# Moving the gate projection of a state-space block into the steps of its scan, with smaller edits to the attention before it

## The reference, cut to what matters

```
s_lat = einsum(q, k) * scale + bias;  s_lat = where(valid, s_lat, -1e30)
p = softmax(concat([s_lat, s_ctx, (sink)]));  out = p_lat @ v + p_ctx @ v_ctx
```

```
u = rmsnorm(h);  lru_x, lru_g, z, xbc, dt = split(u @ w_in)
xbc = silu(causal_conv(xbc));  xs, B, C = split(xbc);  dt = softplus(dt + bias)
y = ssd_scan(xs, dt, -exp(a_log), B, C) + xs * D
g = y * silu(z);  g = g * rsqrt(mean(g*g over each group of 512) + eps) * w
h = h + concat([y_a, g]) @ w_out
```

## Time and profile before

| what | us |
|---|---|
| median of three runs (3709.3 to 3714.8) | 3712.28 |
| the profiled execution, its own time | 3710.25 |
| its span, first to last instruction | 3708.5 |
| mean granted TensorE clock | 0.969 of full |

### The profile page before, as it was taken

How to read it: one execution, slowest core, us unless ns; L and a number is a source line. 1 busy time by engine, 2 the same in 40 slices (tenths; PEclk the granted TensorE clock), 3 DMA queues, 4 the chain that set the end, 5 groups by cost and what they waited for, 6 DMA issues and landing times.

```text
span 3708.5 us, 52151 instructions
## 1 busy us (share of the span) xinstructions
PE 3490.8 (94%) x19951; PEld 3021.8 (81%) x19951; DVE 2211.7 (60%) x3314; ACT 1434.8 (39%) x2472; POOL 724.3 (20%) x299
## 2 busy tenths in 40 slices
PE   7899999988999999999999998899998889979998
PEld 4899997855789999889999785778888789669776
DVE  6888885158288888788888617431226544551065
ACT  4433333147353333453333416542223623321274
POOL 1011111200211111111111230234442134023402
PEclk9999999999999999999999999999998999879999
DMA  5333333110133333333333320123332122012301
GB/s 222 107 121 122 124 104 119 59 46 1 45 140 121 117 119 120 116 119 114 114 114 108 120 74 34 46 69 97 96 102 86 40 79 86 12 46 80 97 7 57
DMA packets 94532, 333.57 MB, mean 90 GB/s; under 512 B 12272, under 2 KB 14576, under 8 KB 93424
## 3 DMA queue, kind: packets, MB, share of 16 engines
q1 hardware_dynamic: 91248, 316.28, 25.6%
q10 hardware_dynamic: 3072, 14.40, 1.1%
HBM read 322.12 MB, written 8.52 MB: 89 GB/s over the span
## 4 chain that ended last, share of the span: by engine, by line
PE 61%; issue 23%; POOL 6%; DVE 6%; ACT 2%; DMA 1%; SPq 0%; POOLq 0%; DVEq 0%; ACTq 0%
PE psum L2374 23%; PE psum L2253 14%; PE psum L2233 13%; POOL w_parts L682 6%; PE psum L2288 1%; PE psum L2131 1%; PE psum L2477 1%; PE psum L2583 1%; DVE normed L1323 1%; PE psum L2680 1%; PE psum L2711 1%; PE psum L2725 1%; PE psum L2707 1%; PE psum L2451 0%; DMA const<-const_dram 0%
## 5 line engine op out<-in xcount | busy, mean ns | idle before, releaser
L682 POOL TENSOR_TENSOR w_parts<-w_raw,w_parts 128x1024 fp32r<-128x1024 f32 x289 | 705.4, 2442 | 2880.7 <-ACT w_parts L722 2867.7
L2233 PE MATMUL psum<-h_parts,w_parts 128*128 128x264 f32 (+1 forms) x5712 | 958.0, 330 | 36.7 <-DVE to_split L1932 10.9
L2233 PEld LDWEIGHTS psum<-h_parts,w_parts 128*128 128x128 f32 x5712 | 854.9, 191 | 135.1 <-issue 34.6
L722 ACT ACTIVATE w_parts<-w_raw 128x1024 fp32r<-128x1024 f32 x283 | 300.1, 1061 | 1113.0 <-PE psum L2233 712.8
L2253 PE MATMUL psum<-w_parts,hidden_parts 128*128 128x512 f32 x2904 | 670.4, 392 | 14.7 <-DVE hidden_parts L1283 7.8
L2253 PEld LDWEIGHTS psum<-w_parts,hidden_parts 128*128 128x128 f32 x2904 | 546.8, 189 | 133.8 <-issue 12.7
L2374 PE MATMUL psum<-h_parts,w_parts 128*128 128x384 f32 x2880 | 531.2, 336 | 16.5 <-ACT y_tok L873 14.1
L2374 PEld LDWEIGHTS psum<-h_parts,w_parts 128*128 128x128 f32 x2880 | 504.5, 189 | 20.4 <-issue 16.9
L892 ACT ACTIVATE w_parts<-psum 128x512 fp32r<-128x512 f32 x240 | 143.8, 599 | 368.3 <-PE psum L2374 145.2
L2374 PE MATMUL psum<-h_sums,w_parts 128*128 128x384 f32 x1440 | 268.9, 334 | 0.0
L2374 PEld LDWEIGHTS psum<-h_sums,w_parts 128*128 128x128 f32 x1440 | 251.3, 188 | 0.0
(11 more groups left out here) (362 smaller groups left out, 4163.7 us busy)
## 6 DMA issues: line engine op xcount, KB each, us to landing
w_raw<-wu_dram SPq DMA_DIRECT2D x295, 512.0 KB, 3.6
mod_ring<-modw_dram SPq DMA_DIRECT2D x128, 512.0 KB, 4.5
w_raw_pairs<-wg_dram SPq DMA_DIRECT2D x120, 512.0 KB, 3.7
kept_dram<-resid SPq DMA_DIRECT2D x2, 3136.0 KB, 9.9
resid<-kept_dram SPq DMA_DIRECT2D x16, 392.0 KB, 5.7
na_bias<-rpb_dram ACTq DMA_DIRECT2D x6, 896.0 KB, 4.8
four_dft<-four_dram ACTq DMA_DIRECT2D x2, 2048.0 KB, 8.3
mod_first_k<-modw_dram SPq DMA_DIRECT2D x7, 512.0 KB, 10.0
```

Of the source, the lines that this page charges most:

```text
L682: pool.tensor_tensor(SPL[:, s % 2, 1], RAW[:, s % 2], SPL[:, s % 2, 0].bitcast(F32), ALU.subtract).then_inc(w_split, 1)
L722: act.activation(SPL[:, u % 2, 0], RAW[:, u % 2], ACT.Copy).then_inc(w_hi, 1)
L2233: ins = pe.matmul(PS[:, pair, PSO[a]:PSO[a] + z - a], w[:, wp, k], src[:, xp, k, t0 + a:t0 + z], start=k == 0 and n_ == 0, stop=k == KT - ...
```

## The change

1. The eight units of z leave their place ahead of the preparation. Each is run as two halves of 264 tokens in scan steps 0 to 7: PE runs the first half after `from_state` and the second after `outputs`, each in one PSUM bank (banks 2 and 3). The decays rotate over two banks instead of three.
2. Silu of z becomes: ACT takes tanh(z/2) into `ZT`, DVE computes (tanh + 1)*z into `Z`, and the gate multiplies by 0.5. The silu instructions and their waits go; a table load for exp and tanh is requested after the last silu of `xbc`.
3. Gating, squares and square sums leave steps 1 to 10 and are done in step 8 (tiles and groups 0 to 3), step 9 (4 to 7) and step 10 (8 and 9), since all of `Z` is needed first.
4. Attention: the row maximum is written negated (`negate=True`), and line 1712 goes.
5. Attention: POOL, not DVE, adds the masks to the second and third bias table of each layer (two instructions a table), after it has split the first 18 units of the layer.

```diff
+    GATE_STEPS = {8: (0, 1, 2, 3), 9: (4, 5, 6, 7), 10: (8, 9)}
...
+            def bias_masks(sub):                                     # POOL
+                mx = sub["in"]["mix"]
+                pool.wait_ge(tab_in, 64 * (mx + 1))
+                for ot in (1, 2):
+                    pool.wait_ge(tb_in[ot % 2], 16 * (mx + 1 if ot == 1 else 2 * mx + 2))
+                    tb = TB[:, ot % 2].rearrange("p x (n r c) -> p x n r c", n=7, r=8)
+                    for x in range(2):
+                        pool.tensor_tensor(tb[:, x], tb[:, x], MASKS[:, 0:7 * NA_C]...broadcast_to([P, 7, 8, NA_C]), ALU.add).then_inc(s_bias, 1)
...
-                for j in unit_steps(u, 8):                            # ACT
-                    act.activation(row2(Z[:, j]), two(u + j), ACT.Silu).then_inc(silu_ready, 1)
-                u += 8
+                act.preload_act_table_set("exp_and_others")
...
+                def z_tanh_half(n):
+                    if n % 2 == 0:
+                        act.wait_ge(z_half, n // 2 + 1)
+                    else:
+                        act.wait_ge(unit_done, u + n // 2 + 1)
+                    if n >= 2:
+                        act.wait_ge(z_read, n - 1)
+                    act.activation(ZT[:, n % 2], bank(2 + n % 2, T2 // 2), ACT.Tanh, scale=0.5).then_inc(z_tanh, 1)
+                decays(*SSD_STEPS[0])
                 for c in range(11):
-                    if c < 10:
-                        decays(*SSD_STEPS[c])
-                    if c >= 1:
-                        gated_squares(*SSD_STEPS[c - 1])
+                    if c < 8:
+                        z_tanh_half(2 * c)
+                    if c < 9:
+                        decays(*SSD_STEPS[c + 1])
+                    if c < 8:
+                        z_tanh_half(2 * c + 1)
+                        high_part(u, 0, c + 2)
+                    for d in GATE_STEPS.get(c, ()):
+                        gated_squares(*SSD_STEPS[d])
...
-                        step(dve.reduce_max(SM[:, a % 2, 0, :], sb[:, :, lo:1 + w + CTX], AX_X))       # DVE
-                        dve.tensor_scalar(SM[:, a % 2, 1, :], SM[:, a % 2, 0, :], -1.0, None, ALU.mult).then_inc(s_max, 1)
+                        dve.reduce_max(SM[:, a % 2, 0, :], sb[:, :, lo:1 + w + CTX], AX_X, negate=True).then_inc(s_max, 1)
...
+                def gate(c, i, g, a, z):
                     dve.wait_ge(y_read, c + 1)
-                    dve.tensor_tensor(x, x, Z[:, 4 * g:4 * g + 4, a:z], ALU.mult).then_inc(gated, 1)
+                    dve.scalar_tensor_tensor(x, x, 0.5, Z[:, 4 * g:4 * g + 4, a:z], ALU.mult, ALU.mult).then_inc(gated, 1)
+                def z_silu_half(n):
+                    j, w = n // 2, T2 // 2
+                    dve.wait_ge(z_tanh, n + 1)
+                    dve.scalar_tensor_tensor(Z[:, j, n % 2 * w:n % 2 * w + w], ZT[:, n % 2], 1.0, bank(2 + n % 2, w),
+                                             ALU.add, ALU.mult).then_inc(z_read, 1)
...
+                    if 1 <= c <= 8:
+                        z_silu_half(2 * c - 1)
                     if c >= 1:
                         gated_out(*SSD_STEPS[c - 1])
+                    if c == 8:
+                        dve.wait_ge(z_read, 16)
+                    for d in GATE_STEPS.get(c, ()):
+                        gate(*SSD_STEPS[d])
                     if c < 8:
+                        z_silu_half(2 * c)
                         dve.wait_ge(s_mm_, c + 1)
...
-                loop_units(u, 2, H2, T2, [(pad_ready, PRIME + 17 + j) for j in range(4)], (silu_ready, SI2 + 8))   # PE
-                u += 8
-                pe.wait_ge(silu_ready, SI2 + 16)
+                pe.wait_ge(pad_ready, PRIME + 20)
...
+                def z_unit_half(n):
+                    j, w = n // 2, T2 // 2
+                    if n % 2 == 0:
+                        pe.wait_ge(w_split, u + j + 1)
+                    if n >= 2:
+                        pe.wait_ge(z_read, n - 1)
+                    parts, a = SPL[:, (u + j) % 2], n % 2 * w
+                    for k in range(DT):
+                        for n_, (wp, xp) in enumerate(((0, 0), (0, 1), (1, 0))):
+                            ins = pe.matmul(bank(2 + n % 2, w), parts[:, wp, k], H2[:, xp, k, a:a + w],
+                                            start=k == 0 and n_ == 0, stop=k == DT - 1 and n_ == 2)
+                    ins.then_inc(unit_done if n % 2 else z_half, 1)
...
                     if c < 9:
                         decays(*SSD_STEPS[c + 1])
                         from_state(*SSD_STEPS[c + 1])
+                    if c < 8:
+                        z_unit_half(2 * c)
                     if c < 10:
                         to_state(*SSD_STEPS[c])
                         outputs(*SSD_STEPS[c])
-                    if c >= 1:
-                        square_sums(*SSD_STEPS[c - 1])
+                    if c < 8:
+                        z_unit_half(2 * c + 1)
+                    for d in GATE_STEPS.get(c, ()):
+                        square_sums(*SSD_STEPS[d])
```

More of the change, by code:

```diff
@@ L206, in build @@
     ST = place("stats", [P, 4, 8], F32)
-    SM = place("softmax_stats", [P, 2, 4, 2], F32)
+    SM = place("softmax_stats", [P, 2, 3, 2], F32)
     LAM = place("lru_rates", [P, 8, 8], F32, a_cond)
@@ L235, in build @@
     COLS = place("ssd_cols", [P, 4, 5, HEADS], F32, a_arena + 47680)
+    ZT = place("z_tanh_half", [P, 2, T2 // 2], F32, LOW)
     XDT = place("ssd_xdt", [P, 5, D], F32, a_y)
@@ L329, in build @@
     four_a_s, four_ev, four_b_s = sem("four_a"), sem("four_read"), sem("four_b")
+    s_bias = sem("bias_masked")
     s_lat, s_out, vf_ready, vf_rows = sem("score_bias"), sem("pv_read"), sem("v_features_ready"), sem("v_rows_mm")
@@ L347, in build @@
         sem("ssd_gated"), sem("ssd_sq_ready"), sem("ssd_sq_summed"))
+    z_half, z_tanh, z_read = sem("z_half_mm"), sem("z_tanh"), sem("z_half_read")
     ssd_const, tile_diag, tile_decay_mm = sem("ssd_const"), sem("ssd_tile_diag"), sem("ssd_tile_decay_mm")
@@ L692, in low_parts @@
                     low_part(u + s, s)
+            def bias_masks(sub):
[5 more added lines that the diff above has]
+                    for x in range(2):
+                        pool.tensor_tensor(tb[:, x], tb[:, x], MASKS[:, 0:7 * NA_C].rearrange("p (n c) -> p n c", n=7).unsqueeze(2)
+                                           .broadcast_to([P, 7, 8, NA_C]), ALU.add).then_inc(s_bias, 1)
             u = 0
             for sub in subs:
+                if sub["kind"] == "mix":
+                    start = sub["in"]["u"] + 18
+                    low_parts(u, start - u)
+                    bias_masks(sub)
+                    u = start
                 if sub["fo"] is None:
@@ L1686, in mix @@
                         sb, w, ot = SB[:, a % 3], st["w"], st["ot"]
-                        if st["na"] and st["t"] == 0:
-                            dve.wait_ge(tb_in[ot % 2], 16 * (mx + 1 if ot == 1 else 2 * mx + 1 + ot // 2))
+                        if st["na"] and st["t"] == 0 and ot > 0:
+                            dve.wait_ge(s_bias, 4 * mx + 2 * ot)
+                        if st["na"] and st["t"] == 0 and ot == 0:
+                            dve.wait_ge(tb_in[0], 16 * (2 * mx + 1))
                             for x in range(2):
@@ L1716, in mix @@
                         dve.wait_ge(s_exp, a + 1)
-                        step(dve.reciprocal(SM[:, a % 2, 3, :], SM[:, a % 2, 2, :]))
+                        step(dve.reciprocal(SM[:, a % 2, 2, :], SM[:, a % 2, 1, :]))
                         for x in range(2):
                             sb = SB[:, a % 3, x, 1:1 + w]
-                            dve.tensor_scalar(sb, sb, SM[:, a % 2, 3, x:x + 1], None, ALU.mult).then_inc(s_norm, 1)
+                            dve.tensor_scalar(sb, sb, SM[:, a % 2, 2, x:x + 1], None, ALU.mult).then_inc(s_norm, 1)
                     if 0 <= i - 2 < N and steps[i - 2]["last"]:
@@ L2033, in sb_out @@
                 dve.wait_ge(sb_pv, m + 1)
-                dve.wait_ge(silu_ready, SI2 + 24)
+                dve.wait_ge(silu_ready, SI2 + 16)
                 v_free(e + m)
@@ L2571, in decays @@
                         q = 2 * c + x
-                        if q >= 3:
-                            pe.wait_ge(e_ready, q - 2)
-                        seg = bank(q % 3).rearrange("p (h t) -> p h t", t=P)
+                        if q >= 2:
+                            pe.wait_ge(e_ready, q - 1)
+                        seg = bank(q % 2).rearrange("p (h t) -> p h t", t=P)
                         if R == P:
@@ L2620, in outputs @@
                     ins.then_inc(ssd_y, 1)
+                def z_unit_half(n):
[10 more added lines that the diff above has]
+                    ins.then_inc(unit_done if n % 2 else z_half, 1)
                 def square_sums(c, i, g, a, z):
                     R = z - a
+                    if c == 0:
+                        pe.wait_ge(z_read, 16)
                     pe.wait_ge(sqy_ready, c + 1)
```

(4 more changed lines are left out.)

6 lines of the change are left out of this document (4 added, 2 removed).

## The result

The changed kernel takes 3717.78 us (median of 20 runs), the kernel before 3712.89 in the same 20 rounds: a ratio of 1.0014, 95% interval 1.0008 to 1.0020, so by the ratio 5.2 us slower (3.0 to 7.4). The forecast was +2.1, no change within 0.2%.

The account below looks back on a forecast made before the run. TensorE was taken to bound the kernel, busy in 94% of the span, with no idle time in the scan for z. State-space +5.7 and attention -3.6 gave +2.1 on 3712.28, so 3714.4 us; range 3701 to 3728.

Parts of the forecast that it names:

- seam: From the last unit ahead of the preparation to the scan's first decay product: +5.2 us (3.5 to 7.1).
- end: After the last z half: square sums in a row, partly at low clock, one wait gone; +4.0 us (-1.5 to +7).
- the state-space part: Sum of the forecast's terms for moving z into the scan and gating behind it: +5.7 us.
- attention: Both attention stages, negated maximum and masks on POOL together: -3.6 us.
- low clock at the start of the scan: First decays and first z half in the scan: 4.7 us lost in place of 9.0, so -4.3 (-6.0 to -1.5).
- later falls: Clock falls after the six later full sets of decays: two to three, 3.8 us lost against 3.0, +0.8 (-3.0 to +6).
- z halves not hidden: In the scan, PE stopping at each of 16 z halves for ACT and DVE: costed at nothing; as rival 14 us, chance 0.04.
- negation: Attention, line 1712 gone from the chain in nine first-stage and six second-stage places: -2.8 us (0 to -11.4).
- masks: Attention, mask additions moved to POOL: -3.2 us off the chain, +2.4 for blocked DVE scalings, together -0.8.
- the first rival: Low clock lasts through seam and scan: 3723.0 us; decides once four sets of decays fall; chance 0.27.
- The signs: Expected in the changed profile: a scan of some 120 us, its start at clock 0.5 for under 10 us.
- The rival that z keeps the clock up: In the scan, no clock falls but the first, and square sums at full clock: 3701.7 us, faster; chance 0.15.

Follow-up runs that it names:

- The 64 and 128 rows: The kernel before with decay products over 64 or 128 rows instead of 16: 3705.25 us (0.9979) with 64, 3695.7 us (0.9950) with 128.
- full rows: Decay products over 128 rows instead of 16: on the changed kernel 3701.44 us (0.9971 to the kernel before), on the kernel before 3695.7 us (0.9950).

## Why the prediction was right, and where it was off

The whole was in range and of the right sign, +2.1 against +5.2 (3.0 to 7.4), and the mechanism held: the scan had no idle time on PE into which z could go, and what changed was the seam, the clock and the end. That it came out so near is in part luck. In the pair of profiles the state-space part comes to +11.3, twice the 5.7 of the forecast (its own run gives +6.7, 3.3 to 10), and attention gained more than forecast, which makes up for a part of it. Term by term, from the pair of profiles for the state-space part and from runs for attention:

| term | forecast | found |
|---|---|---|
| seam | +5.2 | +4.2 |
| low clock at the start of the scan | -4.3 | -3.0 |
| later falls | +0.8 | +3.1 |
| end | +4.0 | +7.0 |
| z halves not hidden | 0 | 0 |
| negation | -2.8 | -5.2 (-8.5 to -1.5) |
| masks | -0.8 | -0.4 (-3.7 to +3.0) |

*The seam.* The copies start at 3108.27, 6.3 us behind the last unit's end (3101.93), paced by the last taps as forecast. The low clock there cost less than I took, +0.7 and not +1.7: two stretches of 3.4 us. It rose at 3114.4, when PE had run nothing but transposes since 3110.2. The Trainium skill ("TensorE: Matmul & The Clock Gate", Part 4: PE-mode transpose) has transposes not counted as activity that brings full clock. The trace disagrees, for these f32 transposes (the page's times are for bf16).

*The start.* From 3119.56 the two sets of decays take 9.55 us against 5.9 at full clock, the first z half 5.45 against 3.1: 6.0 lost in place of 9.0. I had priced the z half at +1.5 from the output units, which are back at full within 4 us; this one ran low for all its length.

*The later falls* were mis-sized: four, not two to three, at 1.5 to 1.7 us each, 6.4 lost; before, the two steps with a fall took 9.4 against 7.75, 3.3. Together with the start, the low clock in the steps cost as much as before (-3.0 and +3.1), where I had it 3.5 cheaper. Four sets was the point from which the first rival was to decide. It came halfway: four falls of six and a first z half at the low clock, but transposes that cost less than forecast, and the whole stayed under 0.2%. The 64 and 128 rows show the cause: the few rows of the decay products.

*The end* was the largest miss. I took one sum at full clock and seven at 1.4 to 1.6 us; all eight were low, at 1.74, and a wait of 1.91 us stood ahead of them where I had let one of 0.99 go. The 80 products take 14.7 us against some 7.7 before, by their starts; sums and wait make +7.9, and the rest of the +7.0, which is the balance of the stage, is small pieces that I have not followed. Why the clock is low from the first sum on stays open: neither the wait nor the single column was shown to be the reason.

*The halves* hide, as forecast: apart from the 1.91 us ahead of the sums, PE is idle for 0.15 us of the scan.

*Attention.* From the start of a maximum to the next reciprocal on DVE it takes 1.41 us where it took 1.60, the 0.19 as priced. I counted 15 places, nine on the chain of the first stage and six by proportion; -5.2 would be 27, though its interval takes in the 15 too. In the profiles of the kernel before and of the negation alone the first stage, from its first maximum to its last reciprocal, takes 136.9 and 134.6 us, the second 99.4 and 97.2, so the second gains as much as the first. POOL stopped DVE in two places, beside the third table's masks of each layer, as counted. Of 120 scalings four are longer there, two of them 2.36 us against 0.55; the four together lose 4.1 us, where I took 2.4.

*The signs.* The clock was low for 13.6 us at the start, not for under 10. The scan of "some 120 us" does not follow from my own terms, which give 81.2 + 46.9 - 4.3 + 0.8 + 4.0 = 128.6; it took 135.1.

The rival that z keeps the clock up fails: dense halves beside the decays did not prevent a fall, full rows did, with z or without.

## What to carry to other kernels

Work moved into a stretch where TensorE is already busy saves nothing there; ask first what makes that stretch slow, and try to take that away in place. Here it was products over 16 of 128 rows; rows of zeros cost no time and gave 17.8 us, a third of it through shorter sets of decays and the rest through the clock, more than any rearrangement tried here. A reduction made of one-column products belongs between dense work, with its operand ready ahead: the same sum took 0.81 us there and 1.74 in a row at the end, at the low clock.

## What the hardware showed that I had not expected

- A product with 16 or 64 rows between products with 128 delays them: the half set of decays takes 1.49 to 1.52 us with 16 or 64 rows and 1.12 with 128, all at full clock. Within the run of eight the starts are equally close (0.11 us); the difference lies where the row count changes (mask to first product 0.41 against 0.32 us, first product to next mask 1.08 against 0.80). The weight loads (PEld) show it too, in the kernel before and with full rows:

```profile
3209.01 0.96 PEld L2583 LDWEIGHTS psum<-ssd_cum,const 16*128 16x128 f32 x8 [0.24 <-issue]
3198.71 1.09 PEld L2584 LDWEIGHTS psum<-ssd_cum,const 128*128 128x128 f32 x8
```

  With 16 rows the first load starts 0.41 us behind the mask product's start (3208.60), together with its own product; with 128 it starts 0.08 us behind it (3198.63), beside the mask product.
- The clock went with the rows of the decay products: with 16 it was 0.50 for 20 us at the scan's start though PE had no gap there, and for some 27 to 30 us of the steps in each of four profiles; with 64 it fell twice for 3.4 us; with 128 it stayed at full through the steps of full tiles.
- At the low clock a product with 64 columns costs as much as one with a single column (6.96 and 6.95 us for 32), as long as its weights have 128 columns. The last 16 products of the later run have weights of 16 columns (the tile of 16 tokens), and that run takes 8.91 us with 64 columns against 7.77 with one.
